# Prompt attention with two heads at once on the halves of TensorE, and a layer norm root by logarithm and exponential

## The chip, the cores and the metric

The kernel runs on one core of one Trainium2 chip. The metric is the device time of one execution in microseconds (us). Five engines work from their own instruction streams and meet at semaphores: PE (TensorE, matmuls and transposes into PSUM), DVE (VectorE), ACT (ScalarE), POOL (GpSimd) and SP (SyncE, which issues most DMAs here). Everything is fp32; a large product is made of three products of rounded high and low parts (`fp32r`), a small one is a plain fp32 matmul, which stands in the trace as two instructions.

## The reference, cut to what matters

Two layers of a decoder trunk on a prompt of 512 tokens and 8 samples of 4 new tokens with 2048 cached tokens each. The parts that the change touches:

```python
# layer 0, prompt: 8 heads x 64, causal, in blocks of 128 queries
s = einsum('bqhd,bkhd->bhqk', q, k) * HEAD_DIM ** -0.5
s = s + (cq[..., :, None] - ck[..., None, :])      # sums of log forget gates
s = where(k_pos <= q_pos, s, -inf)
out = einsum('bhqk,bkhd->bqhd', softmax(s), v)
# layer 1: layer norm over 1024 channels inside the Conformer module
xc = x - mean(x)
y = xc * rsqrt(mean(xc * xc) + EPS)
y = silu(y * g + b) @ w_pw2
```

Beside the prompt's attention, layer 0 attends from the 32 sample tokens over 128 cached pages of 128 tokens (16 a sample), and it projects the input of a gated convolution (the "gates": 12 slabs of 128 channels).

## The kernel before, in words

All activations are held with channels on the partitions: 8 chunks of 128 channels by 544 tokens (512 prompt, 32 sample). A projection is a loop over slabs of 128 output channels.

Layer 0's attention is one long stage of 20 **rounds** (`for n in range(NROUND)`, on every engine). The order in a round is written out by hand, and each engine's loop has the same order of matching steps. What a round does on PE:

- `score_group(n)` (line 1945, rounds 0 to 15): the scores of 8 cached pages, as 64 small matmuls on 32x8 pieces of the array. It waits for DVE's transposes of those pages' keys (`key_turned`, line 1291): there are two for each group, `key_turned(n+1, 0)` near the start of DVE's round n and `key_turned(n+1, 1)` after its gate work.
- `new_scores` in even rounds (line 1964).
- `keys_back(n)` (line 1953): 8 transposes of the scores, after ACT's copy out of PSUM (`scored`, line 941).
- `value_page` (line 2003): 8 pages of cached values, four before and four after the gate work.
- `gate_half(q, n)` (line 2070): half a slab of the gates, 24 matmuls of 256 or 288 columns. `gate_halves` says which halves lie in which round.
- The prompt's attention. It has 32 **blocks** k (8 heads by 4 blocks of 128 queries; a block of query block w has w+1 blocks of keys). In a round two blocks are handled, k0 = 2n and k1 = 2n+1, at two places. A block takes these steps: `block_score` (PE, line 2020), `bias` (DVE, lines 1353, 1356, 1359: add the forget sums, mask, find the maximum), `block_exp` (ACT, line 956), `block_inverse` (DVE, line 1365), `block_scaled` (POOL, line 697), `block_turn` (PE transposes, line 2030), `block_turned` (ACT, line 950, into `pt`), `block_value` (PE, line 2043), and for each pair of heads one `attended` (ACT, line 962).

DVE's round n: `key_turned(n+1, 0)`, the logits of the pages (1377), in odd rounds `shift` (1401), `bias(2n)`, then for each gate half `half_scaled` (1443) and, once a slab is whole, `gate_out` (1456, or 1458, 1461 and 1463), `block_inverse(2n)`, `key_turned(n+1, 1)`, convolution taps and small steps, `bias(2n+1)`. PE's block_score of k1 stands at the end of its round, that of k0 ahead of the first four value pages.

The score and the turned block share one PSUM bank (`p_bank`), the values of four blocks of a pair of heads gather in another (`pv_bank`). SP loads the next keys and values while the round runs (lines 463 and 478), each waiting for its buffer.

The layer norm of layer 1 stands between the convolution and the projection pw2. DVE writes the variance (1747), ACT takes its square root (1126), DVE takes the reciprocal (1756), and then for each of 8 chunks m: DVE multiplies (1762), ACT applies silu (1131) and rounds to the high part (1133), DVE subtracts the offset of the next chunk (`centred`, 1752) and makes the low part (1767). PE's first two slabs of pw2 (`two_slabs`, line 1815) start when chunk 0 is there.

Of the kernel before, what the change touches and what calls it, by code (L numbers as in the profile page):

```python
# [47 lines left out]
BLOCKS = 4 * NH  # L48

# [105 lines left out]
def build(nc, a, o):  # L155
# [6 lines left out]
    with ExitStack() as ctx:  # L162
# [86 lines left out]
        pt, _ = place("pt", [P, TP], F32, ss_at + 4096)  # L249
        cb, _ = place("cb", [P, TP], F32, ss_at + 8192)  # L250
# [46 lines left out]
        gate_bank = lambda q: banks[:, 5 if q == 1 else 7, 224:512] if q % 2 else banks[:, q // 2 % 4, 256:512]  # L297
        x_turned = [banks[:, n:n + 2, :].rearrange("p k c -> p (k c)")[:, 0:T] for n in (0, 4, 2, 6)]
        p_bank, pv_bank = pair[1][:, 0, :], pair[1][:, 1, :]
# [110 lines left out]
        def _(sp):  # L410
# [111 lines left out]
            def head_cum(h):  # L522

                if h:
                    sp.wait_ge(s_sbr, 4 * h)
# [3 lines left out]
                sp.dma_start(cb[:, :], cum_rows[h:h + 1, :].to_broadcast([P, TP])).then_inc(s_cb, 16)  # L529
# [109 lines left out]
        def _(pool):  # L639
# [167 lines left out]
        def _(act):  # L807
# [28 lines left out]
            def root(k):  # L836
# [3 lines left out]
                act.wait_ge(s_rt, k + 1 if k < SQ["var"] else k)  # L840
# [103 lines left out]
            def block_turned(k):  # L944

                w = k % 4
                act.wait_ge(s_tr, k + 1)
                if k:
                    act.wait_ge(s_po, k)
                A(pt[:, 0:(w + 1) * P], p_bank[:, 0:(w + 1) * P], ACT.Copy).then_inc(s_ev, 1)  # L950

            def block_exp(k):

                w, n = k % 4, (k % 4 + 1) * P
                act.wait_ge(s_sb, k + 1)
                A(sb[:, k % 2, 0:n], sb[:, k % 2, 0:n], ACT.Exp, bias=rmax[:, w:w + 1],
                  accum_out=rsum[:, w:w + 1]).then_inc(s_pe, 1)
# [1363 lines left out]
```

## Time and profile before

| | us |
|---|---|
| median of 3 runs | 1497.15 |
| lowest and highest | 1491.23, 1504.64 |
| the profiled execution, its own time | 1493.16 |
| its span, first to last instruction | 1491.4 |
| PE busy | 1424.2 (95%) |
| DVE busy | 720.7 (48%) |
| ACT busy | 470.7 (32%) |
| POOL busy | 595.9 (40%) |

The busy shares are means over stages that differ. The attention rounds run from 123.3 us (the first score group) to about 400 us of the span, the layer norm stands at 1015 to 1025 us. A time in the rows below counts from the span's start; in a timeline, the bracket at a row's end is the idle time of that engine just before it, and who ended it.

### The profile page before, as it was taken

How to read it: one execution, taken by the hardware profiler on the slowest of the kernel's cores; microseconds unless marked ns; L12 is line 12 of the kernel's file. 1: busy time of each engine (PE TensorE's matmuls, PEld its weight loads, DVE VectorE, ACT ScalarE, POOL GpSimd, SP SyncE). 2: the span in 40 equal slices, each digit the busy share in tenths (PEclk: the TensorE clock that was granted, in tenths of full speed). 3: DMA queues.
4: the chain of work that ended last, by engine and by line, in shares of the span. 5: the costliest groups of instructions: out<-in, count | busy, mean ns of one | idle time of the engine just before them, and what ended most of it. 6: DMA issues, size and time to landing. Idle time of an engine off the chain costs nothing. (4 is left out here: it accounts for less than half of the span.)

```text
span 1491.4 us, 34706 instructions
## 1 busy us (share of the span) xinstructions
PE 1424.2 (95%) x14005; PEld 1316.6 (88%) x14005; DVE 720.7 (48%) x1257; ACT 470.7 (32%) x676; POOL 595.9 (40%) x329
## 2 busy tenths in 40 slices
PE   6998999999899999999999999997999999999998
PEld 5897767666899999999999988866999999999998
DVE  5645677676534544104443367668455440144411
ACT  4374222232234222312223331116343421122221
POOL 2322232222333554444553454431445554455441
PEclk9999999999999999999999999998999999999999
DMA  6415879897722332232222446650322223322122
GB/s 181 128 53 182 259 271 340 286 303 254 239 85 63 99 93 69 86 105 85 85 64 70 138 129 165 156 151 16 110 72 84 84 74 95 113 84 86 53 80 74
DMA packets 246246, 192.56 MB, mean 129 GB/s; under 512 B 12129, under 2 KB 205106, under 8 KB 246058
## 3 DMA queue, kind: packets, MB, share of 16 engines
q1 hardware_dynamic: 244561, 188.31, 41.4%
q10 hardware_dynamic: 1181, 1.44, 0.4%
q0 software_dynamic: 400, 1.32, 0.3%
q8 instruction: 77, 1.26, 0.3%
q14 instruction: 27, 0.22, 0.0%
HBM read 173.03 MB, written 6.04 MB: 120 GB/s over the span
## 5 line engine op out<-in xcount | busy, mean ns | idle before, releaser
L676 POOL TENSOR_TENSOR w_l<-w_raw,w_h 128x1024 fp32r<-128x1024 f32 (+2 forms) x195 | 440.9, 2263 | 417.8 <-ACT w_h L823 396.5
L1798 PE MATMUL banks<-xa_h,w_h 128*128 128x272 f32 x1856 | 387.9, 290 | 4.4 <-DVE tmp L1619 3.3
L1798 PE MATMUL banks<-xa_h,w_l 128*128 128x272 f32 x1856 | 384.7, 289 | 0.0
L1798 PE MATMUL banks<-xa_l,w_h 128*128 128x272 f32 x1856 | 383.5, 288 | 0.0
L1798 PEld LDWEIGHTS banks<-xa_h,w_h 128*128 128x128 f32 x1856 | 293.0, 189 | 6.7 <-issue 5.4
L1798 PEld LDWEIGHTS banks<-xa_l,w_h 128*128 128x128 f32 x1856 | 292.4, 189 | 0.0
L1798 PEld LDWEIGHTS banks<-xa_h,w_l 128*128 128x128 f32 x1856 | 290.6, 189 | 0.0
L823 ACT ACTIVATE w_h<-w_raw 128x1024 fp32r<-128x1024 f32 (+2 forms) x193 | 185.1, 961 | 198.7 <-PE banks L1798 198.5
L1798 PE MATMUL banks<-h_h,w_h 128*128 128x272 f32 x928 | 193.6, 290 | 0.3 <-DVE x L1558 0.3
L1798 PE MATMUL banks<-h_h,w_l 128*128 128x272 f32 x928 | 193.0, 290 | 0.0
L1798 PE MATMUL banks<-h_l,w_h 128*128 128x272 f32 x928 | 192.5, 289 | 0.0
L1558 DVE TENSOR_TENSOR x<-banks,x 128x544 f32 (+1 forms) x48 | 34.8, 725 | 266.1 <-PE banks L1798 265.2
L750 POOL TENSOR_TENSOR sr<-sl,r_all 128x544 f32<-128x544 f32 x44 | 59.9, 1362 | 231.4 <-ACT sl L1054 231.4
L1798 PEld LDWEIGHTS banks<-h_h,w_h 128*128 128x128 f32 x928 | 147.0, 190 | 0.8 <-issue 0.6
L1798 PEld LDWEIGHTS banks<-h_l,w_h 128*128 128x128 f32 x928 | 147.0, 190 | 0.0
L1798 PEld LDWEIGHTS banks<-h_h,w_l 128*128 128x128 f32 x928 | 145.9, 190 | 0.0
L1054 ACT ACTIVATE sl<-cv 128x544 f32<-128x544 f32 x44 | 29.0, 659 | 276.2 <-DVE cv L1614 276.2
L697 POOL TENSOR_SCALAR sb<-sb,small 128x128 f32<-128x128 f32 (+3 forms) x32 | 34.7, 1085 | 173.4 <-DVE small L1365 173.4
L1619 DVE TENSOR_TENSOR tmp<-banks,sr 128x544 f32<-128x544 f32 x44 | 31.9, 725 | 107.1 <-POOL sr L750 107.1
L1181 DVE TENSOR_TENSOR gate<-banks,r_all 128x544 f32<-128x544 f32 x44 | 31.8, 723 | 105.1 <-PE banks L1798 99.3
L1291 DVE STREAM_TRANSPOSE k_grp<-k_grp 128x2048 f32<-128x2048 f32 x32 | 73.5, 2298 | 0.5 <-DMA k_grp<-in_cache_k 0.5
L1605 DVE SCALAR_TENSOR_TENSOR cv<-gate,params,cv 128x511 f32<-128x511 f32 x88 | 66.1, 751 | 12.7
(301 smaller groups left out, 1688.1 us busy)
## 6 DMA issues: line engine op xcount, KB each, us to landing
w_raw<-in_w_up SPq DMA_DIRECT2D x88, 512.0 KB, 3.7
k_grp<-in_cache_k SPq DMA_DIRECT2D x128, 256.0 KB, 4.2
v_pg<-in_cache_v SPq DMA_DIRECT2D x120, 256.0 KB, 5.2
w_raw<-in_w_in SPq DMA_DIRECT2D x24, 512.0 KB, 6.1
w_raw<-in_w_down SPq DMA_DIRECT2D x32, 384.0 KB, 3.1
w_raw<-in_w_pw SPq DMA_DIRECT2D x24, 512.0 KB, 3.7
w_raw<-in_w_down SPq DMA_DIRECT2D x32, 320.0 KB, 3.0
w_raw<-in_w_out SPq DMA_DIRECT2D x8, 512.0 KB, 5.1
```

Source lines behind the costliest of these rows:

```text
L676: g.tensor_tensor(w_l[:, slot, 0:n], w_raw[:, slot, 0:n], w_h[:, slot, 0:n].bitcast(F32), ALU.subtract).then_inc(s_lo, 1)
L697: g.tensor_scalar(sb[:, k % 2, 0:n], sb[:, k % 2, 0:n], rinv[:, w:w + 1], None, ALU.mult).then_inc(s_pn, 1)
L750: g.tensor_tensor(sr[:, j // 2, :], sl[:, j // 2, :], r_all[:, :], ALU.mult)\
L823: A(w_h[:, slot, 0:n], w_raw[:, slot, 0:n], ACT.Copy).then_inc(s_hi, 1)
L1054: A(sl[:, b, :], cv[:, b, :], ACT.Silu).then_inc(s_sl, 1)
L1181: V.tensor_tensor(halves(dst), gview(b), halves(r_all[:, :]), ALU.mult).then_inc(s_free, 1)
L1291: V.transpose(k_grp[slot][:, at, :].rearrange("p g x -> p (g x)"), k_grp[slot][:, at, :].rearrange("p g x -> p (g x)")).then_inc(s_tk, 1)
L1558: V.tensor_tensor(halves(flat(x[:, ds(m, 1), :])), gview(q % 2), halves(flat(x[:, ds(m, 1), :])), ALU.add).then_inc(s_xnew, 1)
L1605: V.scalar_tensor_tensor(yp, gate[:, b, 0:TP - n], w, yp, ALU.mult, ALU.add)\
L1619: V.tensor_tensor(halves(tmp[:, b, :]), gview(1), halves(sr[:, b, :]), ALU.mult).then_inc(s_free, 1)
L1798: ins = mm(out[:, half, 0:HT], w, v[:, half * HT:(half + 1) * HT], start=first and t == 0 and n == 0, stop=last and t == phase.tiles - 1 a ...
```

## The change

It has two parts.

**Heads in pairs.** Blocks are numbered anew: `head_block(k)` gives head 2(k//8) + k%2 and query block k%8//2, so that blocks 2n and 2n+1 are the same query block of two neighbouring heads, whose 64 channels lie on partitions 0 to 63 and 64 to 127. Both scores of a pair are issued one behind the other (`pair_scored`), each into its own PSUM bank, and the matmuls of both value products alternate (`pair_valued`), one writing partitions 0 to 63 and the other 64 to 127. Everything of a pair stands at one place of the round: on PE both turns before the page scores come back, both values after them, both scores after the first four value pages and ahead of the gate half. The bank of the values is gone: a block's scores, its turned weights and its output go through one bank each, so a pair's score now waits until ACT has copied the outputs of the pair before it (`attended`, now once a block). `pt` and `cb` (the forget sums of a head) exist twice. Since gate half 1 no longer has a bank of its own in round 0, the gate halves move: round 0 has one instead of two, round 1 none instead of one, round 4 two instead of one, round 18 two instead of one; in rounds 5 to 15 the one half has the other parity.

**The root.** ACT takes `Ln(var + eps)` and then `Exp(-0.5 * ...)` where it took `Sqrt`, and DVE's reciprocal is gone. DVE subtracts the offset from chunks 0, 1 and 2 while it waits, instead of chunk 0 alone.

```diff
+def head_block(k):
+    return 2 * (k // 8) + k % 2, k % 8 // 2
...
-    out = {0: ((0,), (1,)), 1: ((2,), ()), 2: ((3,), (4,)), 3: ((5,), (6,)), 16: ((19,), (20,)), 17: ((21,), (22,)),
-           18: ((23,), ())}
-    for n in range(4, 16):
-        out[n] = ((n + 3,), ())
+    out = {0: ((0,), ()), 2: ((1,), (2,)), 3: ((3,), (4,)), 4: ((5,), (6,)), 16: ((18,), (19,)), 17: ((20,), (21,)),
+           18: ((22,), (23,))}
+    for n in range(5, 16):
+        out[n] = ((n + 2,), ())
...
-    p_bank, pv_bank = pair[1][:, 0, :], pair[1][:, 1, :]
+    p_bank = [pair[1][:, 0, :], pair[1][:, 1, :]]
...
 # POOL, each round
-                if 0 <= 2 * n - 1 < BLOCKS:
-                    block_scaled(2 * n - 1)
...
+                if n < PAIRS:
                     block_scaled(2 * n)
+                    block_scaled(2 * n + 1)
...
 # ACT, each round
+                if 1 <= n <= PAIRS:
                     block_turned(2 * n - 2)
+                    block_turned(2 * n - 1)
+                    attended(2 * n - 2)
+                    attended(2 * n - 1)
...
+                if n < PAIRS:
                     block_exp(2 * n)
+                    block_exp(2 * n + 1)
...
-            A(inv_std, inv_std, ACT.Sqrt, bias=eps[:, :]).then_inc(s_r, 1)
+            A(inv_std, inv_std, ACT.Ln, bias=eps[:, :]).then_inc(s_rt, 1)
+            act.wait_ge(s_rt, SQ["var"] + 1)
+            A(inv_std, inv_std, ACT.Exp, scale=-0.5).then_inc(s_r, 1)
...
 # DVE, each round
-                if 0 <= 2 * n - 1 < BLOCKS:
-                    block_inverse(2 * n - 1)
...
-                if 2 * n < BLOCKS:
+                if n < PAIRS:
                     bias(2 * n)
+                    bias(2 * n + 1)
                 for q in halves_in(n):
                     half_scaled(q)
                     gate_out(q)
-                if 2 * n < BLOCKS:
+                if n < PAIRS:
                     block_inverse(2 * n)
+                    block_inverse(2 * n + 1)
                 if more:
                     key_turned(n + 1, 1)
...
-                if 2 * n + 1 < BLOCKS:
-                    bias(2 * n + 1)
...
-            centred(0)
+            for m in range(3):
+                centred(m)
             dve.wait_ge(s_r, SQ["var"] + 1)
-            V.reciprocal(inv_std, inv_std).then_inc(s_dve, 1)
...
-                if m + 1 < DC:
-                    centred(m + 1)
+                if 3 <= m + 2 < DC:
+                    centred(m + 2)
...
 # PE
+            def pair_scored(n):
+                for k in (2 * n, 2 * n + 1):
+                    h, w = head_block(k)
+                    rows = slice(HD * (h % 2), HD * (h % 2) + HD)
+                    if k >= 2:
+                        pe.wait_ge(s_pod, k - 1)
+                    mm(p_bank[k % 2][:, 0:(w + 1) * P], qkv[rows, h // 2, w * P:(w + 1) * P],
+                       qkv[rows, 4 + h // 2, 0:(w + 1) * P], start=True, stop=True).then_inc(s_s, 1)
...
+            def pair_valued(n):
+                w = head_block(2 * n)[1]
+                pe.wait_ge(s_ev, 2 * n + 2)
                 for kb in range(w + 1):
+                    for k in (2 * n, 2 * n + 1):
+                        h = head_block(k)[0]
+                        ins = mm(p_bank[k % 2][HD * (h % 2):HD * (h % 2) + HD, 0:P], v_tok[:, kb, h * HD:(h + 1) * HD],
+                                 pt[k % 2][:, kb * P:(kb + 1) * P], start=kb == 0, stop=kb == w)
+                        if kb == w:
+                            ins.then_inc(s_po, 1)
```

PE's order in round 13, from its score group to the next one (`k_grp,q_blk`), before. `xa_h,w_h` is the first row of the gate half, whose other 23 rows are left out; `ident,sb` are turns, `pt,v_tok` values, `qkv` alone scores, `v_pg,pr` value pages.

```order
L1945 MATMUL banks<-k_grp_87,q_blk 8x256 x64
L2030 MATMUL banks<-ident,sb 128x128
L1978 MATMUL banks<-small,ones 128x32
L1953 MATMUL banks<-ident,s_t 128x128 x8
L2043 MATMUL banks<-pt,v_tok 64x128
L2020 MATMUL banks<-qkv 128x384
...
L2070 MATMUL banks<-xa_h,w_h 128x256
...
L2030 MATMUL banks<-ident,sb 128x128 x2
...
L2043 MATMUL banks<-pt,v_tok 64x128 x2
L2020 MATMUL banks<-qkv 128x512
L1945 MATMUL banks<-k_grp_86,q_blk 8x256 x64
```

And with the change:

```order
L1951 MATMUL banks<-k_grp_87,q_blk 8x256 x64
L2032 MATMUL banks<-ident,sb 128x128 x2
L1984 MATMUL banks<-small,ones 128x32
L1959 MATMUL banks<-ident,s_t 128x128 x8
L2042 MATMUL banks<-pt_121,v_tok 64x128
L2042 MATMUL banks<-pt_122,v_tok 64x128
...
L2025 MATMUL banks<-qkv 128x256 x2
L2070 MATMUL banks<-xa_h,w_h 128x288
...
L2009 MATMUL banks<-v_pg_96,pr 8x128 x4
L1951 MATMUL banks<-k_grp_86,q_blk 8x256 x64
```

Behind the gate half a turn, a value and a score are gone; only the four value pages are left there ahead of the next score group.

DVE's order around the same place, from the logits' shift of round 13 to the key transposes that end it, before (`sb<-banks` is the first step of a bias, `uh<-banks` the gate half's scaling):

```order
L1401 TENSOR_TENSOR sc_b<-sc_b,banks 128x544
L1353 SCALAR_TENSOR_TENSOR sb<-banks,small,cb 128x384
L1356 TENSOR_TENSOR sb<-sb,causal 128x128
L1359 TENSOR_REDUCE small<-sb 128x1
L1443 TENSOR_TENSOR uh<-banks,r_all 128x256
L1365 RECIPROCAL small<-small 128x1
L1291 STREAM_TRANSPOSE k_grp_86<-k_grp_86 128x2048
```

And with the change:

```order
L1411 TENSOR_TENSOR sc_b<-sc_b,banks 128x544
L1363 SCALAR_TENSOR_TENSOR sb<-banks,small,cb_123 128x256
...
L1363 SCALAR_TENSOR_TENSOR sb<-banks,small,cb_124 128x256
L1366 TENSOR_TENSOR sb<-sb,causal 128x128
L1369 TENSOR_REDUCE small<-sb 128x1
L1453 TENSOR_TENSOR uh<-banks,r_all 128x288
L1468 TENSOR_TENSOR uc<-uc,uh 128x544
...
L1375 RECIPROCAL small<-small 128x1 x2
L1300 STREAM_TRANSPOSE k_grp_86<-k_grp_86 128x2048
```

The second bias has come ahead of the gate half and the key transposes, and in odd rounds the finished slab's work (`uc<-uc,uh` and what follows it) stands there too.

ACT's order at the layer norm, before:

```order
L1124 ACTIVATE sq<-ua 128x544
L1126 ACT_TABLE_LOAD
L1126 ACTIVATE sg<-sg,eps 128x544
L1131 ACT_TABLE_LOAD
L1131 ACTIVATE tmp<-yc,params 128x544
```

And with the change:

```order
L1131 ACTIVATE sq<-ua 128x544
L1133 ACT_TABLE_LOAD
L1133 ACTIVATE sg<-sg,eps 128x544
L1135 ACT_TABLE_LOAD
L1135 ACTIVATE sg<-sg 128x544
L1140 ACT_TABLE_LOAD
L1140 ACTIVATE tmp<-yc,params 128x544
```

There is one more activation and one more table load, between the logarithm and the exponential.

## Rows read from the trace of the kernel before

**Rows 1.** Stretches: us, busy us (instructions) of PE, PEld, DVE, ACT, POOL; PEclk, DMA, GB/s.
```profile
123.29:400.00 276.71, 252.16 (x4345) 191.00 (x4344) 189.03 (x349) 78.54 (x155) 77.65 (x56) 0.96 0.84 281
205.42:352.87 147.45, 137.36 (x2577) 99.70 (x2576) 111.51 (x208) 39.56 (x83) 38.26 (x30) 0.98 0.89 305
246.46:261.57 15.11, 14.32 (x278) 10.88 (x277) 12.31 (x23) 4.85 (x9) 4.01 (x3) 1.00 1.04 368
275.34:294.66 19.32, 17.40 (x277) 12.81 (x276) 11.52 (x22) 4.19 (x8) 4.50 (x3) 0.82 0.94 324
324.33:337.56 13.23, 12.36 (x241) 8.65 (x240) 11.81 (x24) 3.43 (x8) 4.02 (x4) 1.00 0.87 285
```

**Rows 2.** Timeline of PE in odd round 13: start us, us, engine, line.
```profile
329.46 0.43 PE L2043 MATMUL banks<-pt,v_tok 128*64 128x128 f32 x2
329.83 0.91 PE L2020 MATMUL banks<-qkv 64*128 64x384 f32 x2
330.67 1.06 PE L2003 MATMUL banks<-v_pg,pr 128*8 128x128 f32 x32
331.66 0.38 PE L2070 MATMUL banks<-xa_h,w_h 128*128 128x256 f32 x1
...
334.60 0.38 PE L2030 MATMUL banks<-ident,sb 128*128 128x128 f32 x2
334.91 1.06 PE L2003 MATMUL banks<-v_pg,pr 128*8 128x128 f32 x32
335.90 0.65 PE L2043 MATMUL banks<-pt,v_tok 128*64 128x128 f32 x4
336.48 1.12 PE L2020 MATMUL banks<-qkv 64*128 64x512 f32 x2
```

**Rows 3.** Timeline of DVE in round 13, beside the rows above.
```profile
331.71 0.60 DVE L1353 SCALAR_TENSOR_TENSOR sb<-banks,small,cb 128x384 f32<-128x384 f32 x1
...
334.80 0.42 DVE L1443 TENSOR_TENSOR uh<-banks,r_all 128x256 f32<-128x256 f32 x1 [1.18 <-PE banks L2070]
...
335.21 2.29 DVE L1291 STREAM_TRANSPOSE k_grp<-k_grp 128x2048 f32<-128x2048 f32 x1
```

**Rows 4.** Waits of PE's weight loads in all rounds: us in total, times, longest.
```profile
PEld banks L1945 <- DVE k_grp L1291: 11.2, 13, 2.0
```

**Rows 5.** Timeline of PE, end of round 14 and start of round 15.
```profile
348.78 0.60 PE L2030 MATMUL banks<-ident,sb 128*128 128x128 f32 x4
...
352.87 2.67 PE L1945 MATMUL banks<-k_grp,q_blk 32*8 32x256 f32 x128
...
356.65 1.09 PE L1953 MATMUL banks<-ident,s_t 128*128 128x128 f32 x8 [0.52 <-ACT s_t L941]
```

**Rows 6.** Timeline of DVE in round 12, where a slab is finished.
```profile
320.99 0.73 DVE L1458 TENSOR_TENSOR uc<-uc,uh 128x544 f32<-128x544 f32 x1
...
321.98 2.29 DVE L1291 STREAM_TRANSPOSE k_grp<-k_grp 128x2048 f32<-128x2048 f32 x1
```

**Rows 7.** The page's groups: POOL's scaling of the blocks.
```profile
L697 POOL TENSOR_SCALAR sb<-sb,small 128x128 f32<-128x128 f32 (+3 forms) x32 | 34.7, 1085 | 173.4 <-DVE small L1365 173.4
```

**Rows 8.** Waits of PE's matmuls in all rounds: us in total, times, longest.
```profile
PE banks L1953 <- issue: 1.4, 1, 1.4
```

**Rows 9.** Timeline of ACT at the layer norm.
```profile
1016.95 0.75 ACT L1126 ACTIVATE sg<-sg,eps 128x544 f32<-128x544 f32 x1 [0.87 <-DVE sg L1747]
...
1022.08 0.84 ACT L1131 ACTIVATE tmp<-yc,params 128x544 f32<-128x544 f32 x1 [3.08 <-DVE yc L1762]
```

**Rows 10.** Timeline of DVE at the layer norm: the reciprocal.
```profile
1017.73 3.55 DVE L1756 RECIPROCAL sg<-sg 128x544 f32<-128x544 f32 x1 [0.18 <-ACT sg L1126]
```

**Rows 11.** Timeline of PE at the layer norm: the start of pw2.
```profile
1024.85 0.79 PE L1815 MATMUL banks<-h_h,w_h 128*128 128x272 f32 x2 [7.97 <-DVE h_l L1767]
```

**Rows 12.** Timeline of ACT at another norm's logarithm and exponential.
```profile
461.39 1.28 ACT L841 ACT_TABLE_LOAD   x1
462.68 0.66 ACT L841 ACTIVATE r_all<-r_all 128x544 f32<-128x544 f32 x1
```

More of the change, by code:

```diff
@@ L48 @@
 BLOCKS = 4 * NH
+PAIRS = BLOCKS // 2
+def head_block(k):
+    return 2 * (k // 8) + k % 2, k % 8 // 2
 class Steps:
@@ L248, in build @@
         sb, _ = place("sb", [P, 2, TP], F32, ss_at)
-        pt, _ = place("pt", [P, TP], F32, ss_at + 4096)
-        cb, _ = place("cb", [P, TP], F32, ss_at + 8192)
+        pt = [place(f"pt{n}", [P, TP], F32, at)[0] for n, at in enumerate((ss_at + 4096, hl_at + 3 * CH))]
+        cb = [place(f"cb{n}", [P, TP], F32, at)[0] for n, at in enumerate((ss_at + 8192, hh_at + 3 * CH))]
         m1, gmax, diag = small[:, 0:32], small[0:32, 32:33], small[0:32, 64:96]
@@ L528, in head_cum @@
                     sp.wait_ge(s_qk, 8)
-                sp.dma_start(cb[:, :], cum_rows[h:h + 1, :].to_broadcast([P, TP])).then_inc(s_cb, 16)
+                for h in (2 * c, 2 * c + 1):
+                    sp.dma_start(cb[h % 2][:, :], cum_rows[h:h + 1, :].to_broadcast([P, TP])).then_inc(s_cb, 16)
             sp.wait_ge(s_cum, 1)
@@ L535, in _ @@
             for n in range(NROUND):
-                if n % 2 == 0 and n // 2 < NH:
-                    head_cum(n // 2)
+                if n % 4 == 0 and n < PAIRS:
+                    head_cums(n // 4)
                 values_at = GRP * (n - LAG + 1)
@@ L944, in block_turned, with attended @@
             def block_turned(k):
[L946 removed]
+                n = (head_block(k)[1] + 1) * P
                 act.wait_ge(s_tr, k + 1)
[L948 to L950 removed]
+                if k >= 2:
+                    act.wait_ge(s_po, k - 1)
+                A(pt[k % 2][:, 0:n], p_bank[k % 2][:, 0:n], ACT.Copy).then_inc(s_ev, 1)
             def block_exp(k):
[L954 removed]
+                r, n = k % 4, (head_block(k)[1] + 1) * P
                 act.wait_ge(s_sb, k + 1)
[L956 to L962 removed]
+                A(sb[:, k % 2, 0:n], sb[:, k % 2, 0:n], ACT.Exp, bias=rmax[:, r:r + 1],
+                  accum_out=rsum[:, r:r + 1]).then_inc(s_pe, 1)
+            def attended(k):
+                h, w = head_block(k)
+                rows = slice(HD * (h % 2), HD * (h % 2) + HD)
+                act.wait_ge(s_po, k + 1)
+                A(qkv[rows, h // 2, w * P:(w + 1) * P], p_bank[k % 2][rows, 0:P], ACT.Copy).then_inc(s_pod, 1)
             def batch_exps(b):
@@ L2023, in block_turn @@
             def block_turn(k):
                 pe.wait_ge(s_pn, k + 1)
-                pe.wait_ge(s_sbr, min(k + 2, BLOCKS))
-                if k == BLOCKS - 1:
-                    pe.wait_ge(s_ev, k)
-                for kb in range(k % 4 + 1):
-                    ins = tr(p_bank[:, kb * P:(kb + 1) * P], sb[:, k % 2, kb * P:(kb + 1) * P], ident[:, :])
-                ins.then_inc(s_tr, 1)
-            def block_value(k):
-                h, w = k // 4, k % 4
-                rows = slice(HD * (h % 2), HD * (h % 2) + HD)
-                pe.wait_ge(s_ev, k + 1)
-                if k == 0:
-                    half_read(1)
-                if k % 8 == 0 and k:
-                    pe.wait_ge(s_pod, k // 8)
-                for kb in range(w + 1):
-                    ins = mm(pv_bank[rows, w * P:(w + 1) * P], v_tok[:, kb, h * HD:(h + 1) * HD],
-                             pt[:, kb * P:(kb + 1) * P], start=kb == 0, stop=kb == w)
-                ins.then_inc(s_po, 1)
+                for kb in range(head_block(k)[1] + 1):
+                    ins = tr(p_bank[k % 2][:, kb * P:(kb + 1) * P], sb[:, k % 2, kb * P:(kb + 1) * P], ident[:, :])
@@ L2117, in _ @@
                         value_page(values_at + j)
+                if n == 0:
+                    pe.wait_ge(s_qk, 8)
+                if n < PAIRS:
+                    pair_scored(n)
                 for r in late:
```

80 lines of the change are left out of this document (26 added, 54 removed).

## The prediction

> **What bounds the kernel now.** I read the page first: PE is busy for 95% of the span, so time is won where PE waits, or where its own work shrinks without another wait taking its place. The stretches come next, because the attention stage differs from the rest: over rounds 5 to 14 PE is busy for 137.4 of 147.5 us and DVE for 111.5 [rows 1]. That is a stage with two nearly full engines, and what counts is who waits for whom at the start of a round. The waits of PE's weight loads answer that: in 13 of 16 rounds the score group's first weights wait for DVE's key transposes, 11.2 us in total [rows 4]. The timelines of round 13 show how closely the two are matched. On PE the gate half ends as the turn starts at 334.60, and turn, four pages, value and score bring PE to 337.56, 2.96 us later [rows 2]. On DVE the gate half's scaling starts at 334.80, the reciprocal fits in, and the key transposes start at 335.21 and last 2.29 us, to 337.50 [rows 3]. So DVE needs 2.96 us behind an odd round's gate half too: scaling, reciprocal, transposes, with a semaphore at each end. PE's work there is a cover for DVE's chain and no more.
>
> **Heads in pairs, on PE.** Spacings from start to start give the prices. A score of 384 columns holds PE for 0.84 us (329.83 to 330.67), one of 512 for 1.08 [rows 2]; by 0.21 to 0.24 for 128 columns the four widths are 0.41, 0.63, 0.84, 1.08, mean 0.74. A value product over one block of keys takes 0.37 and over two 0.58 [rows 2], so 0.37, 0.58, 0.80, 1.02, mean 0.69. If the two of a pair run at once, 16 scores and 16 values are saved: 16 x 1.43 = 22.9 us of PE's time. That no trace of before shows for halves of the array; the nearest row is the value pages, 16 matmuls on four column strips as 32 instructions in 0.99 us (330.67 to 331.66), where one block's two instructions of the same 128 columns take 0.22 more [rows 2]: 16 x 0.22 would be 3.5 us, so four strips do run at once. Bounds: 22.9 us saved, or nothing. I take the saving, by that row.
> The Trainium skill, TensorE: Matmul & The Clock Gate, Part 3, says that matmuls start and end in program order; an fp32 score being two instructions, the second head's first would then wait for the first head's second, and a pair would take three quarters of the time of two. The pages, faster than that order would allow, speak against it; by the rule the sum would be some 4 us worse.
>
> **Where the saving goes.** Behind the gate half PE now has the four pages alone, 0.99 us [rows 2], and in even rounds three short steps more, about 1.7 in all. DVE's chain stays, and grows:
> - a second reciprocal, 0.07: 3.03 us in every round.
> - In rounds 7, 9 and 13 the one gate half is now the one that ends a slab, with the product of 0.73 us ahead of the transposes, or 1.0 us with its copies [rows 6]. Before, that fell in even rounds, under PE's longer rest.
> - The second bias stands ahead of the gate half. One bias of 384 columns takes 1.9 us (331.71 to 333.62, where the wait of 1.18 before 334.80 begins) [rows 3]. Two with the second exponential behind them, against 2.9 to 3.3 us of gate half, delay the transposes by about 0.5 in the rounds of 384 and 512 columns.
> Odd rounds 5 to 13 thus take (5 x 3.03 + 2.95 + 1.1) / 5 = 3.84 us from the gate half to the next score group against 2.96. Even rounds take (5 x 3.03 + 3 x 0.5) / 5 = 3.33 against 4.09 (348.78 to 352.87) [rows 5]. Ahead of the gate half PE did one value and one score, 0.37 + 0.84 [rows 2]; now it does a pair of each, mean 1.43, so 0.22 more. The turns that moved there lie under ACT's copy of the page scores (352.87 to 356.65) [rows 5], but for 0.2 us in rounds 8 and 12. Ten rounds: 2.2 + 4.4 - 3.8 + 0.4 = 3.2 us more, less the waits that need not return, such as round 15's 0.52 for ACT [rows 5]; of the 10.1 us that PE is idle in these ten rounds (147.45 - 137.36) [rows 1] I take off 3: about 0.
> The other queues stand clear. POOL scales two blocks in a row, 2 x 1.09 us [rows 7], beside the key transposes and the score group. The pair's score waits for two short output copies on ACT, under the four pages; rounds 1 to 3 have no pages, +2 us. The loads keep their pace, as the rounds do; `cb` comes a round earlier. SP waits for nothing new.
> **Rounds 0 to 4:** round 0 loses a gate half, -3; round 1 trades one for a chain of bias, exponential, reciprocal and transposes with nothing over it, -1; round 4 gains a half and saves on its rest, +2.5; with the +2, about 0. **Rounds 15 to 19** get one gate half more (24 matmuls, 2.9 us from 331.66 to 334.60) [rows 2]: +3, and the removed value product is hidden by the wait for POOL there.
>
> **The clock.** The granted clock was 0.82 over round 10, so about 6.9 of its 19.3 us ran at 1.2 GHz, not 2.4; that round had one wait of 1.4 us [rows 1, 8] and was 4.2 us longer than round 8 [rows 1], 2.8 of it by the clock. Round 13 had shorter waits and kept 1.00 [rows 1]. With the change PE idles 3.84 - 0.99 = 2.9 us ahead of the score group in the mean odd round, some 1.6 in the even ones, 3 to 5 in rounds 1 to 3. I expect the clock to fall in about 8 of these 14 rounds, against one now: the clock of 0.98 over rounds 5 to 14 is round 10's alone, and 0.96 over all rounds makes three or so, of which rounds 0 to 4 have the rest [rows 1]. A fall at a score group lies partly over ACT's fixed copy, so I take 2.3 us, between 1.5 and 2.8: two of the three falls of now lie in those 14 rounds, so 8 x 2.3 - 2 x 2.8 = +13.
> The Trainium skill, the same page, The HAM clock gate, says that idle stretches between bursts of matmuls put the array back to half its clock; that speaks against this change, and round 10 agrees.
>
> **The root.** The square root starts at 1016.95 [rows 9], the reciprocal takes 3.55 us [rows 10], silu starts at 1022.08 [rows 9] and PE, after 7.97 us of waiting, at 1024.85 [rows 11]. Now: logarithm 0.75 [rows 9], table load 1.28, exponential 0.66 [rows 12], table load 1.28 again, which the reciprocal covered before: silu at 1016.95 + 0.75 + 1.29 + 0.66 + 1.3 = 1020.95, 1.1 us sooner. The two subtractions moved up take 0.3 more off the first low part: -1.4 (bounds: 0, and 2.5).
> The Trainium skill, ScalarE: Activation LUTs, Table sets, says that logarithm and exponential share a set and need one load. Here a load of 1.28 stands between them [rows 12]; by the page the gain would be 2.7.
>
> **The sum,** on the profiled execution's 1493.2 us (span 1491.4; the median of the runs is 1497.2, 4 above): rounds 5 to 14 0, rounds 0 to 4 0, rounds 15 to 19 +3, clock +13, root -1.4, so 1493.2 + 14.6 = 1507.8. Some of the waits of before that go, above all those for `cb` and in rounds 0 to 4, are not in it; I take off 2: **1506 us**.
>
> **Rivals.**
> - *The clock falls in nearly every round*, 12 falls or more at 2.8: +28 instead of +13, 1521 us. This is the slower side; it decides once idle stretches near 3 us always cost the clock. For it: every odd round has one, and 1.4 us was enough once. Against: the score group follows at once, and the clock holds over rounds with shorter waits, as 13 [rows 1].
> - *The waits take the saving, but the clock holds* (4 falls or fewer): 1506 - 13 = 1493, down to 1488.
> - *The transposes give way:* DVE is early enough and PE's saving counts: 1493 - 22.9 + 3 - 1.4 = 1472. For it: DVE waits 1.18 us for the gate half in round 13 [rows 3]. Against: that wait lies ahead of the chain, not in it.
> - *The halves don't overlap,* and the change doesn't do what it says: PE does all of a pair's work ahead of the gate half, 1.43 - 0.36 = 1.1 us more in 16 rounds: 1506 + 17 = 1523.
>
> **Numbers.** Forecast (5 to 11 falls, 1499 to 1514) 0.42; nearly every round 0.21; clock holds 0.20; transposes give way 0.11; no overlap 0.06. The range 1484 to 1524 leaves out the fourth and the far tails. One per cent, 15 us, is what a measurement of this kernel tells from no change. Faster by more (under 1478): 0.11 and a tail of 0.03, 0.14. Slower (over 1508): rival 1 and 4, and 0.14 of the forecast: 0.41. Same: 0.45.
>
> **What would show it.** Right: after the four pages PE's score group waits for `k_grp` by 2 to 3.5 us in odd rounds; rounds 5 to 14 last 145 to 165 us; PE busy falls while the stage doesn't; the granted clock of the stage is 0.83 to 0.92 against 0.96 [rows 1]; two scores of a pair start within 0.1 us; silu starts about 4 us after the logarithm. Wrong: score groups without that wait (transposes), pairs in a row (overlap), or a stage clock near 0.96.

## The result, and the profile of the changed kernel

The changed kernel takes 1506.8 us (median of 17 runs, 1500.0 to 1511.9) against 1497.2 us (17 runs, 1491.2 to 1504.6): 1.0064 times as long, 95% interval 1.0050 to 1.0079. The profiled executions differ by as much: 1502.7 us (span 1500.9) against 1493.2 (span 1491.4), 9.5 us. I forecast 1506. The total is right, but two of its terms were wrong by 8 to 10 us in opposite directions. What follows is read from one profiled execution of each kernel; both of these lie about 4 us under their medians.

First the stretches of the changed kernel (columns as in [rows 1]): rounds 0 to 4, rounds 5 to 14, the last group's scores and all behind them up to the output projection (the *tail*), then rounds 10 and 13 alone, and the first of these lines once more up to 400 us.

```profile
121.11:204.54 83.43, 66.21 (x1061) 49.68 (x1060) 54.62 (x89) 28.29 (x59) 23.49 (x19) 0.86 0.75 247
204.54:352.30 147.76, 123.35 (x2563) 92.24 (x2563) 113.27 (x204) 43.98 (x102) 39.96 (x31) 0.95 0.88 300
352.30:412.02 59.72, 48.31 (x725) 41.18 (x726) 27.25 (x59) 13.18 (x22) 14.89 (x7) 0.91 0.66 216
...
277.15:292.26 15.11, 13.24 (x268) 9.39 (x268) 11.15 (x19) 4.20 (x10) 4.40 (x3) 0.90 0.75 247
322.16:337.28 15.12, 11.22 (x236) 8.22 (x237) 10.27 (x23) 4.61 (x11) 3.33 (x4) 1.00 1.05 386
...
121.11:400.00 278.89, 229.32 (x4214) 175.13 (x4213) 188.71 (x340) 84.80 (x182) 73.63 (x54) 0.92 0.83 277
```

The kernel before, for the two stretches that [rows 1] doesn't have:

```profile
123.29:205.42 82.13, 73.20 (x1085) 56.53 (x1085) 52.02 (x86) 27.51 (x52) 26.59 (x19) 0.92 0.74 247
...
352.87:401.38 48.51, 41.96 (x691) 35.07 (x690) 26.54 (x58) 11.72 (x21) 13.70 (x8) 1.00 0.81 261
```

The 9.5 us are: -2.2 ahead of round 0 (the first input landed sooner in this execution, nothing of the change), +1.3 in rounds 0 to 4, +0.3 in rounds 5 to 14, **+11.2 in the tail**, -1.4 at the layer norm, +0.3 elsewhere. A difference of 1 or 2 us in one stretch is no more than executions of the same code differ by: in the profiled execution of pairs_only (below) rounds 0 to 4 took 81.62 us, not 83.43. In rounds 5 to 14 PE is busy for 14.0 us less (137.36 in [rows 1], 123.35 now) and the stretch is as long as before: the saving is there, and all of it is waiting. Where it waits, the waits of PE's matmuls show:

```profile
PE banks L1951 <- DVE k_grp L1300: 34.5, 15, 4.2
PE banks L1821 <- DVE h_l L1773: 6.5, 1, 6.5
...
PE banks L2016 <- DVE own L1434: 3.5, 1, 3.5
...
PE banks L2001 <- DVE own L1434: 3.3, 1, 3.3
```

L1951 is the score group, L1300 the key transpose: 3.7 us of such waits over all rounds before, 34.5 now. L1821 is the start of pw2, 7.97 us of waiting in [rows 11] and 6.5 now. The two waits for `own` belong to the tail.

Round 13, to be laid beside [rows 2] and [rows 3]. PE:

```profile
329.20 0.70 PE L2025 MATMUL banks<-qkv 64*128 64x256 f32 x4
329.83 0.40 PE L2070 MATMUL banks<-xa_h,w_h 128*128 128x288 f32 x1
...
333.22 1.06 PE L2009 MATMUL banks<-v_pg,pr 128*8 128x128 f32 x32
337.28 3.86 PE L1951 MATMUL banks<-k_grp,q_blk 32*8 32x256 f32 x128 [3.00 <-DVE k_grp L1300]
```

and DVE:

```profile
329.93 0.48 DVE L1363 SCALAR_TENSOR_TENSOR sb<-banks,small,cb 128x256 f32<-128x256 f32 x1 [1.93 <-PE banks L2025]
...
333.33 0.46 DVE L1453 TENSOR_TENSOR uh<-banks,r_all 128x288 f32<-128x288 f32 x1 [0.96 <-PE banks L2070]
333.88 0.73 DVE L1468 TENSOR_TENSOR uc<-uc,uh 128x544 f32<-128x544 f32 x1
334.64 0.18 DVE L1471 COPY ext_a<-uc 128x32 f32<-128x32 f32 x1
334.73 0.16 DVE L1473 COPY tail_a<-uc 128x2 f32<-128x2 f32 x1
334.80 0.22 DVE L1375 RECIPROCAL small<-small 128x1 f32<-128x1 f32 x2
334.94 2.29 DVE L1300 STREAM_TRANSPOSE k_grp<-k_grp 128x2048 f32<-128x2048 f32 x1
```

The gate half ends at 333.22, PE does four pages and waits 3.00 us; DVE goes through scaling, slab product, two copies, reciprocals and transposes, and is done at 337.2. The same rows show the flaw that the experiments use: DVE idles for 1.93 us ahead of the bias, with the transposes still to be done.

### The profile page after: what moved, and what is told of

It reads as the page before. It is cut to its first block and busy times, and to the rows that moved or that the text cites. A ratio compares the mean times of both kernels' runs of the same rounds, so it can differ in the third digit from the quotient of the medians.

```text
span 1500.9 us, 34670 instructions
## 1 busy us (share of the span) xinstructions
PE 1409.4 (94%) x14005; PEld 1306.7 (87%) x14005; DVE 721.5 (48%) x1256; ACT 479.6 (32%) x706; POOL 594.9 (40%) x329
## 3 DMA queue, kind: packets, MB, share of 16 engines
q8 instruction: 77, 1.26, 0.3%
## 5 line engine op out<-in xcount | busy, mean ns | idle before, releaser
L1951 PE MATMUL banks<-k_grp,q_blk 32*8 32x256 f32 x2048 | 53.0, 462 | 34.5 <-DVE k_grp L1300 34.5
L1300 DVE STREAM_TRANSPOSE k_grp<-k_grp 128x2048 f32<-128x2048 f32 x32 | 73.4, 2296 | 1.0 <-DMA k_grp<-in_cache_k 1.0
```

What stands on the lines that cost most here:

```text
L1300: V.transpose(k_grp[slot][:, at, :].rearrange("p g x -> p (g x)"), k_grp[slot][:, at, :].rearrange("p g x -> p (g x)")).then_inc(s_tk, 1)
L1951: ins = mm(raw_scores[32 * c:32 * c + 8, i, :], q_blk[32 * i:32 * i + 32, c, part, b, :], keys[32 * i:32 * i + 32, 4 * c + part, :, :], st ...
```

## The experiments

Ratios are to the kernel before, run beside each, with 95% intervals.

**root_only** and **pairs_only**: one half of the change each.

root_only also drops the reciprocal and moves the subtractions up; pairs_only takes all of it back in the changed kernel.

```diff
-            A(inv_std, inv_std, ACT.Sqrt, bias=eps[:, :]).then_inc(s_r, 1)
+            A(inv_std, inv_std, ACT.Ln, bias=eps[:, :]).then_inc(s_rt, 1)
+            act.wait_ge(s_rt, SQ["var"] + 1)
+            A(inv_std, inv_std, ACT.Exp, scale=-0.5).then_inc(s_r, 1)
```

> The kernel before with the layer norm's root by logarithm and exponential alone. Theory: the gain is that of the changed kernel, where PE's wait at the norm went from 8.24 us (1016.61 to 1024.85) to 6.80 (1027.42 to 1034.22), 1.4 us: 1495.7 us, ratio 0.9990; the rest of the time unmoved. Rival: the two ways cost the same and the 1.4 us came from elsewhere in that stage: ratio 1.000, and PE's wait there stays near 8.2 us.

> The changed kernel with the root and its reciprocal as before, so the pairs of heads alone. Theory: all of the loss is the pairs': 1506.8 + 1.4 = 1508 us, ratio 1.0074 to the kernel before; the attention stage as in the changed kernel (15 waits for the key transposes, 34.5 us, 10 to 12 falls of the clock before 420 us) and PE's wait at the norm back near 8.2 us. Rival: the moved subtractions or the new table loads cost something beside the norm: ratio under 1.006.

Measured: root_only 1494.5 us, 0.9977 (0.9961 to 0.9993); pairs_only 1508.5 us, 1.0065 (1.0044 to 1.0087). PE's waits for pw2's first low part, of root_only and of pairs_only:

```profile
PE banks L1815 <- DVE h_l L1767: 6.5, 1, 6.5
```

```profile
PE banks L1951 <- DVE k_grp L1298: 34.5, 15, 4.3
PE banks L1821 <- DVE h_l L1773: 8.0, 1, 8.0
```

Both came out where they were put. The 1.4 us go with the root and the 34.5 us with the pairs. By the medians the root alone gained 2.7 us; 1.4 lies inside its interval (1.0 to 5.8 us). The rounds and the tail of pairs_only are those of the changed kernel, and show how much executions differ. Its rounds 0 to 4 and 5 to 14:

```profile
122.80:204.42 81.62, 63.25 (x1062) 48.19 (x1061) 54.62 (x89) 28.38 (x59) 23.46 (x19) 0.92 0.79 257
204.42:355.05 150.63, 127.47 (x2564) 95.30 (x2564) 113.68 (x204) 44.38 (x102) 39.87 (x31) 0.92 0.85 291
```

Its tail took 67.5 us, not 59.7; what stands in it is told at values_first.

**keys_early**: the second transpose ahead of the biases, in the changed kernel.

```diff
                 if spread is not None:
                     shift(spread)
+                if more:
+                    key_turned(n + 1, 1)
                 if n < PAIRS:
                     bias(2 * n)
...
                     block_inverse(2 * n + 1)
-                if more:
-                    key_turned(n + 1, 1)
```

> The changed kernel with one step moved on DVE: the second key transpose of the next group (2.29 us) runs ahead of the two biases, not behind the gate half and the reciprocals. Theory (DVE's chain behind the gate half sets the round): DVE idles 1.93 and 1.34 us ahead of the biases of rounds 13 and 14, so the transpose costs the biases 0.4 to 1.0 us there, under 3 us of gate half; the waits of the score groups for the keys go from 34.5 us over 15 rounds to under 8, the stage gets 15 to 30 us shorter (what is late next: POOL's scaling, the landing of the keys), and with shorter waits the clock falls 5 times or fewer: 1480 us, between 1470 and 1492, ratio 0.98 to 0.997. Rival 1 (the transfers set the round, their engines being busy for about 0.87 of the stage): the transposes wait for DMA instead, and the stage loses under 8 us: 1500 or more. Rival 2 (ACT and POOL are as late as DVE): the wait goes to the keys' copies or the turns, 1500 or more, with over 15 us of new waits there.

Measured: **1466.2 us**, 0.9793 (0.9775 to 0.9812), 40.6 us under the changed kernel and below my range. Its rounds 0 to 4, rounds 5 to 14 and tail:

```profile
121.75:187.68 65.93, 59.47 (x1061) 46.88 (x1060) 52.19 (x88) 28.18 (x59) 22.32 (x17) 0.97 0.93 313
187.68:313.44 125.76, 118.13 (x2565) 89.24 (x2564) 113.10 (x202) 43.61 (x101) 40.94 (x31) 1.00 0.98 351
313.44:373.07 59.63, 48.24 (x725) 40.63 (x726) 27.83 (x60) 13.44 (x24) 17.36 (x9) 0.91 0.67 220
```

The group's wait for the transposes is gone from PE's matmuls (0.2 us is left in its weight loads); rounds 0 to 14 are 39.5 us shorter, the 34.5 us of waits and 5 more. That the 5 come from the clock (0.97 and 1.00, not 0.86 and 0.95) is likely, not shown. The tail is unmoved. What bounds these rounds next isn't shown: the transfers are busy for 0.98 of rounds 5 to 14, but PE is busy for 118.1 of the 125.8 us too, and none of its waits there names a transfer. Both rivals fell. This settles the main step of the prediction: DVE's chain held the rounds.

**before_keys_early**: the same edit in the kernel before.

> The kernel before with the same step moved in the same way, ahead of its first bias. Theory: it has 11.2 us of such waits in PE's weight loads and 3.7 in its matmuls; about 4 to 9 us go: 1490 us, ratio 0.994 to 0.998. The pairs' own worth is then this kernel against the changed one with the step moved: 10 to 15 us for the pairs, where PE works and the saving counts. Rival: once the transposes are out of the way both kernels are held by the same other thing (transfers), and they come out within 3 us of each other.

Measured: 1494.3 us, 0.9978 (0.9964 to 0.9991). Rounds 0 to 4 lose 5.2 us and rounds 5 to 14 grow by as much, to 152.67. So in the kernel before, taking the transposes out of the way gives almost nothing, and less than the 4 to 9 us that I expected. Its rounds 5 to 14 are longer in three rounds: 9, 11 and 14 took 16.9, 18.3 and 17.4 us where they had taken 13.8, 13.9 and 15.3, while round 10 fell from 19.3 to 14.8. In 3.9 us of PE's waits ahead of score groups the profile shows nothing that it waited for, so the cause stays open; single long rounds stand in the executions of before and root_only too (19.3 us in round 10, 18.7 in round 14). The rival, both kernels within 3 us of each other, fell: against keys_early it is 28 us behind, 1.4 of it the root: with the transposes early the pairs are worth some 27 us, more than the 10 to 15 that I gave them and than the 22.9 us of matmuls that they save. That the second block's steps at the end of each round went too may be the rest; no run tries it.

**tail**: rounds 16 to 18 get the gate halves that they had before the change.

```diff
-    out = {..., 4: ((5,), (6,)), 16: ((18,), (19,)), 17: ((20,), (21,)), 18: ((22,), (23,))}
-    for n in range(5, 16):
-        out[n] = ((n + 2,), ())
+    out = {..., 4: ((5,), (6,)), 5: ((7,), (8,)), 16: ((19,), (20,)), 17: ((21,), (22,)), 18: ((23,), ())}
+    for n in range(6, 16):
+        out[n] = ((n + 3,), ())
```

> The changed kernel with its gate halves dealt out so that rounds 15 to 19 get what they had in the kernel before (one, two, two and one), and the half that is left over goes to round 5, whose two halves are 7 and 8. Theory: 11.2 of the 9.5 us of difference arose behind the last score group (59.7 us to the output projection against 48.5), 2.9 of it the extra gate half, the rest the order, in which the last slabs' ends come one half later for DVE, and two falls of the clock; so the tail gets 8 to 11 us shorter, round 5 gets 2.9 longer, and the later rounds win up to 3 as the slab's product leaves the odd rounds: 1498 us, between 1495 and 1502, ratio to the kernel before 0.999 to 1.003. Rival: the tail is long because of the pairs (two turns and two values behind one scaling), whatever the halves do: 1504 to 1509.

Measured: 1499.4 us, 1.0016 (0.9995 to 1.0037). Its tail:

```profile
353.82:404.79 50.97, 43.92 (x701) 36.27 (x702) 27.52 (x55) 12.49 (x22) 15.13 (x8) 0.93 0.74 245
```

51.0 us, not 59.7; rounds 5 to 14 got 2.1 longer. Dealing the halves out as before took back 8.7 of the tail's 11.2 us, 2.9 of it the half that went to round 5 and the rest their place. Some 2.5 us stay with the pairs themselves. The theory held (1498 us, between 1495 and 1502).

**values_first**: from round 15 on, a finished batch's values are scaled ahead of sum, taps and low part.

```diff
+                if n >= 15 and valued is not None:
+                    values(valued)
                 if spread is not None:
                     total(spread)
                 for c, k in pieces.get(n, ()):
                     conv_tap(c, k)
...
-                if valued is not None:
+                if n < 15 and valued is not None:
                     values(valued)
```

> The changed kernel with one step moved on DVE from round 15 on: the scaling of a finished batch's values (two of 0.47 us) ahead of the exponentials' sum, the convolution's taps and the low part. It tells whether DVE's order makes the two waits of PE for these values in rounds 18 and 19 (3.3 and 3.5 us). Theory: the first ends 3 us sooner, the second 2.4, and the time falls by 4 to 5.5: 1502 us. Rival: the slab's product (2.46 us) that stands ahead of it in any case holds the wait, or the next wait takes its place (the low parts for the output projection), and the time stays within 2 us of 1507.

Measured: 1499.1 us, 1.0012 (0.9989 to 1.0035), 7.7 us under the changed kernel by the medians. PE's waits in its tail:

```profile
PE banks L1986 <- DVE small L1425: 3.0, 1, 3.0
...
PE banks L2018 <- DVE own L1434: 0.9, 1, 0.9
```

Of the two waits for `own` one is gone and one 0.9, so DVE's order did make them. But a wait of 3.0 for another of DVE's small steps stands in this execution, and its tail is no shorter (60.5 us). That wait, 1.1 us in the changed kernel's profile, is not the edit's doing: pairs_only and keys_one_half have it at 3.0 too. In pairs_only:

```profile
386.87 2.34 POOL L697 TENSOR_TENSOR w_l<-w_raw,w_h 128x1024 fp32r<-128x1024 f32 x1 [12.39 <-ACT w_h L932]
387.18 2.06 DVE L1423 TENSOR_SCALAR small<-small 128x2 f32<-128x2 f32 x1
```

DVE's step took 2.06 us beside POOL's low part (2.10 in values_first); in the changed kernel's profile it took 0.23 at 383.14, just ahead of POOL's step at 383.44. Executions with this wait have tails of 67.5 (pairs_only) and 65.8 (keys_one_half) at clocks of 0.80 and 0.84, those without it 59.3 to 59.7 (changed kernel, keys_early, filler). So like against like the step gained 5 to 7 us, which fits the medians, though each figure is one execution's. How often the changed kernel's unprofiled executions have the long tail isn't known.

**filler**: work that nobody reads, in PE's waits.

```diff
-                pe.wait_ge(s_tk, 2 * n + 2)
...
+                for g in range(0 if not n else 16 if n % 2 == 0 or n < 5 else 10):
+                    tr(key_scores(g % GRP), ident[:, :], ident[:, :])
+                pe.wait_ge(s_tk, 2 * n + 2)
```

> The changed kernel with work that nobody reads in PE's waits for the key transposes: ahead of each score group but the first, PE writes 10 or 16 turned copies of the identity (1.3 or 2.0 us, by 1.02 us for 8) over the banks that the group then fills. It tells what the falls of the clock cost. Theory (a fall costs 1.7 to 2.3 us, as in the prediction): falls between 120 and 400 us go from 11 to 4 or fewer, and the time falls by 7 to 14 us: 1496 us. Rival (the falls lie over waits, and so cost nearly nothing): the falls go, or don't, and the time stays within 3 us of 1507.

Measured: 1504.5 us, 1.0051 (1.0031 to 1.0072). Rounds 0 to 4 and 5 to 14:

```profile
121.41:199.42 78.01, 67.80 (x1136) 54.34 (x1135) 54.38 (x89) 28.08 (x59) 23.50 (x19) 0.98 0.81 268
199.42:348.20 148.78, 135.66 (x2695) 104.09 (x2697) 113.16 (x204) 43.79 (x102) 39.96 (x31) 0.99 0.88 297
```

The granted clock rose from 0.86 and 0.95 to 0.98 and 0.99. A stretch of L us at clock c was at 1.2 GHz for 2 x (1 - c) x L: 23.4 + 14.8 = 38 us of rounds 0 to 14 in the changed kernel, 3.1 + 3.0 = 6 here. These 32 us give back 4.4 (231.2 against 226.8), 0.14 us for each. The two stretches differ: rounds 0 to 4 give back 5.4 for 20 us, rounds 5 to 14 take 1.0 more although 12 us of half clock are gone, so the filler may itself have delayed something there. A second measure has no filler: pairs_only ran the same rounds with 10 us less at 1.2 GHz in rounds 0 to 4 (clock 0.92) and took 1.8 less, with 9 more in rounds 5 to 14 (0.92) and took 2.9 more, 0.18 and 0.31 us for each. I take 0.14, between 0.14 and 0.3. The rival was nearer: the time fell by 2.3 us in the medians, which the intervals don't tell from nothing, and the falls cost little here.

**keys_tail**, **keys_tail2** and **keys_15** deal the halves out differently on keys_early: as in tail; with one more moved forward; and with the spare one in round 15.

keys_tail2 first, then keys_15:

```diff
+    out = {..., 5: ((7,), (8,)), 6: ((9,), (10,)), 16: ((20,), (21,)), 17: ((22,), (23,))}
+    for n in range(7, 16):
+        out[n] = ((n + 4,), ())
...
+    out = {..., 4: ((5,), (6,)), 15: ((17,), (18,)), 16: ((19,), (20,)), 17: ((21,), (22,)), 18: ((23,), ())}
+    for n in range(5, 15):
+        out[n] = ((n + 2,), ())
```

> The changed kernel with the second key transpose early, and the gate halves dealt out as in the run called tail. Theory: both gains add, since one lies in rounds 0 to 14 and the other behind them: 1466.2 - 8 = 1458 us, between 1454 and 1462, ratio 0.974. Rival: the halves cost more where PE has become the bound in the rounds, and the sum is under 4 us: 1462 or more.

> As keys_tail, with one more gate half moved forward (round 6 has halves 9 and 10, rounds 16 and 17 two each, round 18 none). Theory of covers: the last rounds idle for DVE's own chain (total, taps, own heads), which the gate halves cover as well as they can; taking them away there uncovers the waits, while round 6 pays 2.9 us in full: 1458 to 1462 us, no better than keys_tail. Rival: the slabs' ends set the tail, and one more out of it gives 3 to 5 us: 1453 to 1455.

> The kernel keys_early with the gate halves dealt out as in the changed kernel up to round 14, two in round 15 (17 and 18), and from round 16 on as in the kernel before. Theory: rounds 5 to 14 stay at 125.8 us (keys_tail, which put the spare half in round 5 and so turned the order of all later rounds round, took 131.9), and the tail from the last score group on is that of keys_tail, 50.8, plus 2.9 to 3.3 for the spare half, against 60.0: 1466.2 - 6 = 1460 us, between 1457 and 1463. Rival: rounds 5 to 14 of keys_tail were longer by the state of the transfers and not by the order, then 1462 to 1465.

Measured: 1462.6 us, 0.9766 (0.9744 to 0.9788); 1480.0 us, 0.9883 (0.9860 to 0.9907); 1460.1 us, 0.9741 (0.9708 to 0.9774). Rounds 5 to 14 of the three, in this order:

```profile
189.00:320.90 131.90, 121.90 (x2588) 92.48 (x2587) 116.46 (x207) 44.44 (x103) 40.93 (x31) 1.00 0.95 333
```

```profile
187.75:330.66 142.91, 129.71 (x2612) 98.02 (x2612) 116.16 (x209) 45.87 (x104) 44.26 (x33) 0.95 0.92 309
```

```profile
187.67:314.81 127.14, 118.91 (x2564) 89.43 (x2564) 113.27 (x202) 43.67 (x101) 40.87 (x31) 1.00 0.98 348
```

keys_tail's tail is 50.5 us, as short as that of the run called tail, but its ten rounds pay 6.1 us for one half of 2.9: its rival held. keys_15 keeps the rounds (127.1) and has a tail of 54.3, and came out where it was put. keys_tail2 missed by 18 us, against both theories. In its rounds PE waited 6.6 us in three score groups for nothing that the profile shows, the transfers moved 309 GB/s where keys_15 has 348, and the clock was 0.95; I can't say which of these came first.

**keys_one_half**: the price of the overlap, on keys_early.

```diff
-                    mm(p_bank[k % 2][:, 0:(w + 1) * P], qkv[rows, h // 2, w * P:(w + 1) * P],
-                       qkv[rows, 4 + h // 2, 0:(w + 1) * P], start=True, stop=True).then_inc(s_s, 1)
+                    mm(p_bank[k % 2][:, 0:(w + 1) * P], qkv[0:HD, h // 2, w * P:(w + 1) * P],
+                       qkv[0:HD, 4 + h // 2, 0:(w + 1) * P], start=True, stop=True).then_inc(s_s, 1)
```

> The kernel keys_early with both scores of a pair taken from the same 64 rows of the array (the odd head's query and key come from the even head's rows, so the second head's scores are left out and the first's computed twice): the two can't run at once. It prices the overlap where PE, not DVE, sets the rounds. Theory: 16 scores of mean 0.74 us come back, in full, since they lie ahead of the gate half in PE's order: 1466.2 + 11.8 = 1478 us, between 1475 and 1481. Rival 1: half of it is covered by waits that the rounds still have, 1470 to 1473. Rival 2: the overlap was never worth anything, 1466.

Measured: 1474.0 us, 0.9840 (0.9807 to 0.9874), 7.8 us more than keys_early, between the theory and the first rival. A pair of 256 columns from the same rows, and what follows it:

```profile
247.10 1.13 PE L2025 MATMUL banks<-qkv 64*128 64x256 f32 x4
248.16 0.40 PE L2070 MATMUL banks<-xa_h,w_h 128*128 128x288 f32 x1
```

That is 1.06 us, where the pair on both halves takes 0.63 (keys_early) and two scores apart from each other would take 1.26. For 128, 384 and 512 columns it is 0.64, 1.49 and 1.91 against 0.42, 0.84 and 1.06. So the overlap itself is worth 0.54 us a pair in the mean and not the 0.74 of my expectation, 8.6 us in all and not 11.8; the other 0.2 comes from issuing one behind the other. Rounds 5 to 14 take 129.5 us against 125.8 for 5.4 us more of score time: two thirds of it costs. The profiled execution has the long tail (65.8 against 59.6), so what the 7.8 us of the medians hold besides the overlap isn't shown.

**keys_15_values**: keys_15 with the step of values_first.

> keys_15 with the step of values_first. Theory: the two moves partly buy the same waits (with keys_15's halves PE waits only 0.6 and 1.6 us for these values), so of the 7.7 us that the step gave the changed kernel 1 to 2 are left: 1458.5 us, between 1456 and 1460. Rival: what the step gave was not these waits, and it adds in full: 1453 or less.

Measured: 1459.0 us, 0.9751 (0.9728 to 0.9774), no different from keys_15, as the theory had it. These two are the best versions, 37 and 39 us under the kernel before that ran beside each.

## Why the prediction was right, and where it was not

- **PE's saving: right.** A pair of scores of 256 columns holds PE for 0.63 us (329.20 to 329.83), as one did (0.63 by the prediction's list). In a window of PE's timeline that ends at 329.35, both heads' first instructions have started:

```profile
329.20 0.49 PE L2025 MATMUL banks<-qkv 64*128 64x256 f32 x2
```

  The Trainium skill, TensorE: Matmul & The Clock Gate, Part 3, read as in the prediction, would make it three quarters of 1.26, 0.95 us; the measurement decides against that reading. In rounds 5 to 14 PE's busy time fell by 14.0 us, where ten pairs at the prediction's 1.43 make 14.3. (Up to 400 us it fell by 22.8, 252.16 to 229.32, but that is not the saving: the changed kernel has 8.6 us of its work behind 400. From the first score group to the output projection, the same work in both, it fell by 14.7, at a lower clock.) By keys_one_half about 0.2 us of each pair of scores comes from issuing them together, not from the overlap.
- **Where the saving goes: right**, in mechanism and size. Behind the gate half of round 13, DVE's chain and PE's wait of 3.00 us are the ones worked out (2 to 3.5 forecast for odd rounds). The waits behind rounds 5, 7, 9, 11 and 13 are 1.9, 3.0, 2.7, 2.5 and 3.0 us, behind the even rounds 1.4 to 1.7, forecast 1.6. The 1.9 behind round 5 lies just under the forecast. Rounds 5 to 14: +0.3 us, forecast 0 before the clock. keys_early is the proof by removal.
- **The clock: number of falls right, price wrong.** The forecast was 8 falls in rounds 1 to 14. By the clock of each round's stretch it was below 0.95 in exactly 8 of them (1 to 4, 6, 10, 11 and 14). The step that failed is "I take 2.3 us, between 1.5 and 2.8". That price came from round 10 of before, where the clock of 0.82 meant 6.9 us at 1.2 GHz, for 2.8 us of time by the prediction's reading, 0.4 for each. Of the ten rounds from 5 on, the four that fell now had 0.89 or 0.90, some 3.3 us each; and a microsecond at 1.2 GHz costs 0.14 us of time by filler, up to 0.3 by pairs_only. I put that down to the waits that now stand beside it: where DVE's chain ends last, a faster PE waits longer. Rounds 0 to 14 had 19 us at 1.2 GHz before (13.1 + 5.9) and 38 now: 19 x 0.14 = 2.7 us, at most 6, where the sum had 13.
- **The first rival** asked whether idle stretches near 3 us always cost the clock. They don't. These are the score groups of rounds 8, 10, 12 and 14, cut at the window's end:

```profile
247.72 1.14 PE L1951 MATMUL banks<-k_grp,q_blk 32*8 32x256 f32 x43 [3.02 <-DVE k_grp L1300]
```

```profile
277.15 1.44 PE L1951 MATMUL banks<-k_grp,q_blk 32*8 32x256 f32 x33 [2.72 <-DVE k_grp L1300]
```

```profile
308.28 1.09 PE L1951 MATMUL banks<-k_grp,q_blk 32*8 32x256 f32 x40 [2.47 <-DVE k_grp L1300]
```

```profile
337.28 1.83 PE L1951 MATMUL banks<-k_grp,q_blk 32*8 32x256 f32 x66 [3.00 <-DVE k_grp L1300]
```

  Rounds 8 and 12 kept 1.00, 10 and 14 did not. They differ in more than the waits: 8 and 12 have blocks of 128 columns, 10 and 14 of 384. What decides it no run shows.
- **Rounds 15 to 19: wrong, +3 against +11.2.** The step counted the gate half that came in (2.9 us) and took its place in the order for free. The last slabs' second halves now end one half later, so DVE's work behind them starts when PE has only one half left as cover. DVE in rounds 17 and 18:

```profile
391.16 0.46 DVE L1453 TENSOR_TENSOR uh<-banks,r_all 128x288 f32<-128x288 f32 x1 [2.77 <-PE banks L2070]
391.71 2.46 DVE L1468 TENSOR_TENSOR uc<-uc,uh 128x544 f32<-128x544 f32 x1
...
394.37 1.13 DVE L1417 TENSOR_REDUCE small<-pr 128x32 f32<-128x544 f32 x1
...
397.86 0.47 DVE L1434 TENSOR_SCALAR own<-banks,small 128x64 f32<-128x64 f32 x2
```

  PE waits 3.3 us for `own` at 398.47, where it waited about 0.5 before, and 3.5 again at 411.43 (2.2 in two waits before). That is 4 us; with the half's 2.9, the rest, some 4 us, is for the most part the clock, 0.91 over the tail against 1.00. Here a fall is not over a wait: gate half 23 took 4.8 us and not 3.3. The other fall stands at 367 to 377 us, behind PE's waits of 1.9 and 0.9 for POOL's scaling of the last pair, which the pairs bring and not the halves: up to round 16's gate halves the tail is already 3.2 us longer (21.4 against 18.2). values_first and tail confirm the order's part; the clock's part is read from the trace and was not tried.
- **The root: right**, -1.4 forecast, 8.24 to 6.80 us from PE's last step ahead of it to its start. ACT:

```profile
1027.76 0.75 ACT L1133 ACTIVATE sg<-sg,eps 128x544 f32<-128x544 f32 x1 [0.87 <-DVE sg L1755]
1028.53 1.28 ACT L1135 ACT_TABLE_LOAD   x1
1029.82 0.66 ACT L1135 ACTIVATE sg<-sg 128x544 f32<-128x544 f32 x1
1030.49 1.28 ACT L1140 ACT_TABLE_LOAD   x1
1031.79 0.84 ACT L1140 ACTIVATE tmp<-yc,params 128x544 f32<-128x544 f32 x1
```

  Silu starts 4.03 us after the logarithm. The load of 1.28 between logarithm and exponential that the Trainium skill, ScalarE: Activation LUTs, Table sets, would spare is there.

So the sum, with measured terms, is 1493.2 - 2.2 (start) + 2.7 (clock) - 1.1 (rounds 0 to 14 otherwise) + 11.2 (tail) - 1.4 (norm) + 0.3 = 1502.7. The forecast stood by luck: the clock's term was 10 us too big and the tail's 8 too small. More luck is in the base. The sum was made on the profiled execution's 1493.2, and on that base it is 3 us too high (1506 against 1502.7); that the median, 1506.8, meets it so closely comes from the 4 us between profile and median. With 0.3 us for each microsecond at 1.2 GHz the clock's term would be 6 and the rest of rounds 0 to 14 -4, with the same total.

## What to carry to other kernels

Work taken off the busiest engine counts only where the other engine's chain is shorter than what is left; ask for each wait which single instruction of that chain could run in a gap that the same timeline shows; here a step of 2.29 us, moved in each of 15 rounds into idling of 1.93 us (round 13), gave 40 us. When steps are dealt out anew over rounds, follow the last ones to the end by name: there each engine's chain is bare, and the place of a step costs more than its length. And price a low clock by what lies beside it, not by its duration. And a stretch read from one execution can be off by several us (59.7 and 67.5 for the same tail here): look at it in every profile that has the same code before explaining its length.

## What was not expected of the hardware

- DVE's product of two 544-column tiles in SBUF takes 0.73 us at 333.88 and 2.46 at 391.71, where POOL's low part (below) runs; it ends 0.6 us after POOL's. The same happens at 405.33 and 408.50 in this execution, three times 1.7 us. It isn't new with the change: the kernel before has it too, at 386.87 (the second row below) and, 2.24 us long, at 394.28.

```profile
391.21 2.38 POOL L683 TENSOR_TENSOR w_l<-w_raw,w_h 128x1024 fp32r<-128x1024 f32 x1 [5.38 <-PE banks L2070]
```

```profile
386.87 2.48 DVE L1458 TENSOR_TENSOR uc<-uc,uh 128x544 f32<-128x544 f32 x1
```

  The Trainium skill, SBUF — State Buffer, SBUF: two separate sides, says that a DVE instruction with two inputs in SBUF and a GpSimd instruction that reads SBUF take one port pair in turn, the later waiting for the whole of the earlier; the trace agrees, and the scaling at 391.16, which reads PSUM, took its usual 0.46 beside the start of the same instruction. The step of 128x2 that took 2.06 us in pairs_only has a single tile as its input, and waits as well.
- The transfers, 300 GB/s and 0.88 busy in rounds 5 to 14 of the changed kernel, went to 351 GB/s and 0.98 as soon as the rounds asked for it (keys_early): 0.88 was not their limit.
